# Gated delta rule: 20 of a head's 288 projection products change places, and one ScalarE copy moves behind the turned keys

## What is computed

```
gc = cumsum(g);  decay = exp(gc_i - gc_j) for i >= j
lower = (kb @ k.T) * decay            (strictly below the diagonal)
sol   = (I + lower)^-1 @ [v*beta, kb*exp(gc)]  -> u, w
qk    = (q @ k.T) * decay
per chunk:  v_new = u - w @ S
            o     = (q*exp(gc)) @ S + qk @ v_new
            S     = S*exp(g_last) + (k*exp(g_last-gc)).T @ v_new
out = rms(o) * gain * silu(z)
```

## Time and profile before

| | |
|---|---|
| median of 3 runs (1944.55 to 1955.01) | 1945.4 us |
| the profiled execution: its own time, and its span | 1947.46 us, 1946.1 us |
| TensorE matmul busy | 1682.9 us, 86% |
| VectorE, ScalarE, GpSimd busy | 743.8, 549.6, 162.4 us |
| mean granted TensorE clock | 0.913 of full |
| the eight heads of the delta rule | 133.4 to about 702 us of the span |

### The profile page before, as it was taken

How to read it: one execution, slowest core, us unless ns; L and a number is a source line. 1 busy time by engine, 2 the same in 40 slices (tenths; PEclk the granted TensorE clock), 3 DMA queues, 4 the chain that set the end, 5 groups by cost and what they waited for, 6 DMA issues and landing times. The chain is left out here.

```text
span 1946.1 us, 30186 instructions
## 1 busy us (share of the span) xinstructions
PE 1682.9 (86%) x11733; PEld 1487.7 (76%) x11733; DVE 743.8 (38%) x1283; ACT 549.6 (28%) x890; POOL 162.4 (8%) x177
## 2 busy tenths in 40 slices
PE   4899889888898979975569989898987799997996
PEld 2598888888898979864556444457986799997996
DVE  1254554544544422314124334435345433332224
ACT  2243333332332321100002323323132434341222
POOL 0012312312312201100000000000000000000000
PEclk9799989989989977977887989998998899998997
DMA  6423112113202151435443244344212233332211
GB/s 187 116 67 84 57 32 86 54 32 86 64 22 97 44 143 48 147 100 162 135 133 115 76 152 130 108 135 171 87 65 87 63 89 86 87 103 92 86 63 44
DMA packets 228643, 181.70 MB, mean 93 GB/s; under 512 B 8544, under 2 KB 221017, under 8 KB 228370
## 3 DMA queue, kind: packets, MB, share of 16 engines
q1 hardware_dynamic: 203390, 161.82, 27.5%
q10 hardware_dynamic: 25184, 18.96, 3.1%
HBM read 166.31 MB, written 23.02 MB: 97 GB/s over the span
## 5 line engine op out<-in xcount | busy, mean ns | idle before, releaser
L704 PE MATMUL dn_pg<-proj_xh,dn_wh 128*128 128x260 f32 x832 | 183.8, 297 | 5.7 <-DVE dn_wl L1003 5.5
L704 PE MATMUL dn_pg<-proj_xh,dn_wl 128*128 128x260 f32 x832 | 182.5, 296 | 0.0
L704 PE MATMUL dn_pg<-proj_xl,dn_wh 128*128 128x260 f32 x832 | 179.0, 293 | 0.0
L251 PE MATMUL gu_ps<-fh_xh,gu_wh 128*128 128x260 f32 x704 | 142.5, 284 | 19.1 <-DVE gu_wl L310 19.1
L251 PE MATMUL gu_ps<-fh_xh,gu_wl 128*128 128x260 f32 x704 | 142.4, 284 | 0.0
L251 PE MATMUL gu_ps<-fh_xl,gu_wh 128*128 128x260 f32 x704 | 142.3, 284 | 0.0
L704 PEld LDWEIGHTS dn_pg<-proj_xh,dn_wh 128*128 128x128 f32 x832 | 134.3, 195 | 7.3 <-DVE dn_wl L1003 6.4
L704 PEld LDWEIGHTS dn_pg<-proj_xh,dn_wl 128*128 128x128 f32 x832 | 134.2, 195 | 0.0
L704 PEld LDWEIGHTS dn_pg<-proj_xl,dn_wh 128*128 128x128 f32 x832 | 134.0, 195 | 0.0
L251 PEld LDWEIGHTS gu_ps<-fh_xh,gu_wh 128*128 128x128 f32 x704 | 109.2, 190 | 19.5 <-issue 19.5
L251 PEld LDWEIGHTS gu_ps<-fh_xh,gu_wl 128*128 128x128 f32 x704 | 109.1, 189 | 0.0
(11 more groups left out here) (471 smaller groups left out, 3383.9 us busy)
## 6 DMA issues: line engine op xcount, KB each, us to landing
all_ring<-in_w_gu SPq DMA_DIRECT2D x44, 512.0 KB, 5.0
all_ring<-in_w_in SPq DMA_DIRECT2D x32, 512.0 KB, 6.9
att_ada<-in_w_ada SPq DMA_DIRECT2D x16, 1024.0 KB, 5.2
fd_ring<-in_w_down SPq DMA_DIRECT2D x8, 1408.0 KB, 6.3
all_ring<-in_w_in SPq DMA_DIRECT2D x10, 1024.0 KB, 5.4
fr_ada<-in_w_ada SPq DMA_DIRECT2D x8, 1024.0 KB, 8.7
dn_xs<-in_w_in SPq DMA_DIRECT2D x16, 512.0 KB, 3.8
all_ring<-in_cmp_w ACTq DMA_DIRECT2D x16, 512.0 KB, 4.3
```

Source lines behind the costliest of these rows:

```text
L251: last = pe.matmul(self.ps[:, j, c, 0:HALF], w[:, j, k, :], x[:, k0 + k, c * HALF:(c + 1) * HALF], start=(k0 + k == 0 and w is self.wh and ...
L704: last = pe.matmul(pg[:, j, c, 0:HALF], w[:, j, k, :], x[:, k, c * HALF:(c + 1) * HALF], start=(k == 0 and term == 0), stop=(k == KD - 1 a ...
```

## The change

Three numbers of the table `BITES` set how many products stand at which place; the last place takes what is left over. ScalarE's copy of unit 1 moves from ahead of the four copies of the turned keys to behind them.

```
-BITES = {"scaled": 100, "turned": 6, "kk": 12, "hop": 7}
+BITES = {"scaled": 80, "turned": 6, "kk": 22, "hop": 7}
...
                 if more:
                     take(h1, 0)
                     split_high(h1, 2)
-                    take(h1, 1)
                 else:
                     keep_last(0)
                     split_last(2)
-                    keep_last(1)
                 for n, (bank, dst) in enumerate(((Dp, knT), (B, kbT), (A, qnT), (C, qgT))):
                     a.wait_ge(turned, 4 * h + n + 1 + START)
                     a.activation(dst[:], bank[:], ACT.Copy).then_inc(ch_ready, 1)
                 if more:
+                    take(h1, 1)
                     split_high(h1, 3)
                 else:
+                    keep_last(1)
                     split_last(3)
```

## The result

The changed kernel takes 1928.2 us (median of 6 runs, 1925.3 to 1939.0) against 1945.0 us beside it: a ratio of 0.9917, 95% interval 0.9891 to 0.9943, or 16 to 17 us less. The forecast was 1925 us with a range of 1916 to 1938. The profiled execution of the changed kernel is the slowest of the six, 1939.04 us with a span of 1937.7, and the only one above that range; how that comes about is most of what follows.

A forecast was written before the change was run, and what follows sets the result against it. Each head was taken as bounded by the chain of hand-overs, stretched by where the filling products lie. -16.0 + 0 + 0 + 0.3 - 4.85 = -20.6 us, from the median 1945.4 us to 1925 us; range 1916 to 1938 us.

The forecast's parts named there:

- The first bite: Ahead of the key turns, 100 to 80 products: key turns start 1.72 to 2.38 us sooner a head, 16.0 us in all.
- The bite behind the key products: Ahead of line 748, 12 to 22 products: ten more fit into 1.59 us of idle, cost 0.
- The ScalarE copy: Unit 1's copy behind the four key copies: 1.5 us to spare, cost 0, at most 4.8 us in eight heads.
- The last bite: Ahead of the result's turn, 10 to 20 products: 1.6 us stay idle, cost 0, but 0.3 us in head 7.
- The clock behind the turn: Behind the result's turn: full clock at five of seven turns, 0.97 us each, gains 4.85 us; bounds 0 and 7.7.
- rival (a): Behind the result's turn: the clock still falls at every turn, only the sooner key turns remain; 1930 us, chance 0.28.
- (b): At the new wait before the key turns: the clock falls now and then, in four heads; 1935 us, chance 0.09.
- (c): At the wait before the key turns: the clock falls in every head and stays down; 1953 to 1966 us, chance 0.06.
- The levels: Half-clock stretches of 3.40 us in heads 1, 3, 5 left as they are; up to 1.7 us each, -5.1 to +6.8 us.

The follow-up runs named there:

- the key bite's run: Against the kernel before: 90 products ahead of the key turns, 22 behind the key products, 10 ahead of the result's turn; 1929.5 us, ratio 0.9895.
- the two halves: Two runs with 90 products ahead of the key turns, the ten others ahead of the result's turn (1921.9 us) or behind the key products (1929.5 us).
- the end bite's runs: Against the kernel before: 90 products ahead of the key turns, 12 behind the key products, 20 ahead of the result's turn; 1921.9 us, ratio 0.9886.

## Why the prediction was right

**The first bite** came out as worked out: the key turns follow the last scaled tile by 0.06 us, and the new wait is 0.64 us where 0.7 was expected. **The bite behind the key products** cost 0.1 us a head (7.93 for 7.83); its wait fell from 1.59 to 0.41, 0.4 forecast. Of the 0.1 us, 0.06 lie in the first four transposes, which now follow idle and last 0.66 us for 0.60, and 0.03 in VectorE's addition of the identity (1.77 us for 1.74). The 0.24 us a product that I gave for half clock there is too high: in head 2 of the kernel before, two products take 0.43 us at half clock (275.33 to 275.76). With 0.22 us the overrun is 1.5 us, inside the bounds I gave, and no key bite in this profile came under half clock. **The ScalarE copy** cost nothing, shown by the run with it alone. **The last bite** left 1.57 us of idle, 1.6 forecast; the 0.3 us charged to head 7 are not seen, its levels and chunks got shorter.

**The clock behind the turn** stayed up at all seven turns; I had taken five, and rival (a), that it falls at every turn, did not come. First transposes to the turn of the head before are 1.63 us apart. These two terms together are 23.0 us in the profile, summed over the eight heads from the turn (in head 0 from the first transposes) to the key turns, where I had 20.85: 16 us for the first bite as forecast, and 7 us for the clock, a good 1 us a turn at nearly all seven. My reason, that idle of 2.77 us brings the clock down and 1.6 mostly does not, was half right: 2.77 us leaves it up in some runs.

**The key turns at full clock.** Rivals (b) and (c) did not come: 214.90 to 222.80 is at 1.00, with 0.64 us idle in front and 16 transposes at its head, and no head of the three profiles of the changed kernel has half clock there. What the Trainium skill's page "TensorE: Matmul & The Clock Gate" says in "Part 4: PE-mode transpose", that the full clock does not engage for transposes because they are not counted as activity in the same way, shows nowhere in these runs. They do not settle it either, since 2.77 us of plain idle also left the clock up at four turns of the key bite's run. The row that I set against it in the prediction (head 2, 276.20 to 280.00) does not either: behind its 12 transposes stand eight ordinary products of the decay (line 728, from 278.75), and projection products just ahead.

**The levels** are the step that was mis-sized. I wrote that the stretch there "has its own cause (a ScalarE step that stays) and I leave it; each such stretch costs up to 1.7 us". The cause was right as far as the runs go: the stretches go with the wait. The size was not: after the change some of these stretches last 17 us and cost 7.4 us a head, three of them in the first profile, and the levels shifted that execution by 20.7 us where I had allowed 6.8. By heads against before, that execution gained 23.0 us up to the key turns, gave 0.7 back behind them, lost 20.7 in the levels and chunks of heads 0, 3, 5 and 6, and won 4.7 in head 7, whose two stretches of half clock (behind line 748, and in the chunks at 686) are gone: 6.4 us of gain in the stage; 1.7 us lie ahead of it. Without any such stretch the changed kernel would take some 1914 us, an estimate from this execution (1939.0 less two times 1.6 and three times 7.4). The forecast of 1925 is thus near the median in part by luck, for two errors that partly cancel: a gain of some 31 us (1945 to 1914, in which the three short stretches of the kernel before, 4.8 us, count as gone), and a loss that differs from run to run.

What stays open is what decides whether a wait of 1.68 us is followed by no half clock, by 3.4 or by 17 us of it. The length of the wait is one part, shown by 1.18 us (none of 14 heads in two kernels), 1.66 to 1.68 us (24 of 49 heads in seven profiles) and 2.80 us (all seven). It does not set the length of the stretch, and the place of the head in the execution does not either. The stretches of 17 us stand only in the three profiles of the changed kernel, 7 of 21 heads. The profiles of the kernel before, of the copy alone and of the two halves have none in 28 heads with the same wait; but each is one execution, and the end bite's runs spread from 1916.8 to 1938.6 us, so whether the change brings the long stretches on is open as well.

## What to carry to other kernels

Where one engine fills its waits with other work, read the list of waits for the places that are missing from it: no wait at a step of the chain can mean that the filling makes the chain late, and products belong where a wait is listed, no more of them than its length. Waits of 1.7 to 2.8 us can cost twice, once for themselves and once for the clock behind them, and the second share varies from run to run; shortening one such wait of TensorE by a reordered copy gave about as much as the whole change. A spread of runs by a few fixed steps is a reason to read the granted clock head by head.

## What the runs showed of the hardware that was not expected

The same idle at the same place is not always followed by the same clock: 2.77 us before the result's turn left it at 1.00 in four of seven heads of one run, and brought it to 0.50 behind all seven turns of the kernel before. With 1.57 us there it stayed up at 41 of 42 turns in six profiles. Once down in the levels, where short matmuls and hand-overs alternate, it stayed at 1.2 GHz for 17 us although TensorE was busy for 16.31 of 17.00 us there; with a longer wait in the same place it came back after 3 to 7 us.
